# Latent attention: the softmax denominators of two query blocks are copied out by ScalarE, inverted by VectorE as 128 by 8 values and spread over partitions through DRAM

## The reference, cut to what matters

```
def attend(q, k, v):
    s = jnp.einsum('bqhgd,bkhd->bhgqk', q, k, preferred_element_type=jnp.float32) * (HEAD_DIM ** -0.5)
    p = jax.nn.softmax(s, axis=-1).astype(v.dtype)
    return jnp.einsum('bhgqk,bkhd->bqhgd', p, v)
...
    k_all = jnp.concatenate([kc, kl], axis=1)
    v_all = jnp.concatenate([vc, vl], axis=1)
    y_lat = merge(blocked_attention(ql, k_all, v_all), gal, fourier_mix(ul, f_gain, w_fmix), gbl)
```

## Time and profile before

| | |
|---|---|
| median of 3 runs | 3614.19 us (3607.61 to 3617.55) |
| profiled execution | span 3604.0 us; the page gives no other time for it |
| latent attention | about 690 to 1790 us of the span |
| DVE L2456, reciprocal | 24 times, 80.6 us |
| DVE busy over the span | 2375.8 us, 66% |
| ACT busy | 1357.8 us, 38% |
| PE busy | 3380.0 us, 94% |

### The profile page before, as it was taken

The page is one execution under the profiler, slowest core; times in us unless marked ns, Lnnn a source line. Parts: engine busy times, 40 slices in busy tenths (PEclk is TensorE's granted clock), DMA queues, the critical chain, the costliest instruction groups (busy, mean ns, idle before and its releaser), DMA issues. The chain is left out here.

```text
span 3604.0 us, 49705 instructions
## 1 busy us (share of the span) xinstructions
PE 3380.0 (94%) x16176; PEld 2490.9 (69%) x16176; DVE 2375.8 (66%) x3519; ACT 1357.8 (38%) x2274; POOL 1822.6 (51%) x1224
## 2 busy tenths in 40 slices
PE   7999998799999999999889799799999998999798
PEld 5788885555555555555488699687878786877587
DVE  4666544778877777777757654466575645777566
ACT  3433335444444444444320133234343423654200
POOL 1033313477777777777534344333686513444354
PEclk8999998899999999999999899999999999999899
DMA  5335545411111111111255455564545446777563
GB/s 204 116 109 142 142 135 187 147 33 35 36 36 35 36 36 35 35 36 35 94 171 175 160 185 177 181 201 148 170 134 170 152 149 208 219 224 238 191 224 138
DMA packets 358832, 475.35 MB, mean 132 GB/s; under 512 B 57932, under 2 KB 212444, under 8 KB 358512
## 3 DMA queue, kind: packets, MB, share of 16 engines
q1 hardware_dynamic: 300592, 358.80, 32.0%
q10 hardware_dynamic: 51600, 94.16, 8.6%
q0 software_dynamic: 6448, 19.94, 1.4%
HBM read 337.32 MB, written 135.36 MB: 131 GB/s over the span
## 5 line engine op out<-in xcount | busy, mean ns | idle before, releaser
L2413 DVE TENSOR_REDUCE al_mx<-al_sx 128x1 f32<-128x512 f32 (+1 forms) x960 | 559.3, 631 | 202.6 <-PE al_sx L2516 193.2
L2333 ACT ACTIVATE al_e<-al_st 128x1024 f32<-128x1024 f32 x432 | 442.8, 1026 | 536.1 <-PE al_st L2531 534.3
L2382 POOL TENSOR_TENSOR al_acc_p<-al_acc_p,al_e 128x1024 f32<-128x1024 f32 x188 | 455.3, 2422 | 19.8 <-POOL al_acc_p L2382 0.9
L319 PE MATMUL pb_acc<-p_whi,pb_r_hi 128*128 128x512 f32 x952 | 379.0, 398 | 38.7 <-DVE pb_r_lo L1767 28.1
L2540 PE MATMUL al_acc<-al_e,vres 128*64 128x512 f32 x1728 | 402.6, 601 | 0.0
L321 PE MATMUL pb_acc<-p_whi,pb_r_lo 128*128 128x512 f32 x952 | 376.4, 395 | 0.0
L320 PE MATMUL pb_acc<-p_wlo,pb_r_hi 128*128 128x512 f32 x952 | 375.8, 395 | 0.0
L1767 DVE TENSOR_TENSOR pb_r_lo<-pb_stg,pb_r_hi 128x512 fp32r<-128x512 f32 x238 | 247.5, 1043 | 167.6 <-ACT pb_r_hi L1665 163.4
L2530 PE MATMUL al_st<-al_qa,kres 128*128 128x512 f32 x864 | 346.8, 401 | 3.8 <-issue 3.2
L2531 PE MATMUL al_st<-al_qb,kres 128*128 128x512 f32 x864 | 341.0, 395 | 0.0
L2516 PE MATMUL al_sx<-kres,al_qx 128*128 128x512 f32 (+1 forms) x960 | 311.5, 398 | 9.1 <-DVE al_mx L2413 6.9
(11 more groups left out here) (340 smaller groups left out, 7387.0 us busy)
## 6 DMA issues: line engine op xcount, KB each, us to landing
pb_stg<-s_hsum ACTq DMA_DIRECT2D x238, 256.0 KB, 2.8
s_proj<-pb_out SPq DMA_DIRECT2D x72, 256.0 KB, 3.3
p_wst<-in_w1s ACTq DMA_DIRECT2D x18, 1024.0 KB, 5.9
ml_k<-s_proj SPq DMA_DIRECT2D x36, 512.0 KB, 4.4
ml_v<-s_proj SPq DMA_DIRECT2D x36, 512.0 KB, 9.0
hm_w<-in_ada_w SPq DMA_DIRECT2D x16, 1024.0 KB, 7.9
ml_qt<-s_qt SPq DMA_DIRECT2D x32, 512.0 KB, 6.4
s_h<-ml_h POOLq DMA_DIRECT2D x32, 512.0 KB, 8.4
```

The lines of the kernel that those rows point to most:

```text
L319: nc.tensor.matmul(out, s_hi, m_hi, start=start, stop=False)
L2333: nc.scalar.activation(e[:, pair(p, j), :, :], st[(NP * p + j) % 2][:, :, 0:W], ACT.Exp).then_inc(e_done, 1)
L2382: nc.gpsimd.tensor_tensor(acc_p[:], acc_p[:], e[:, pair(p, j)], ALU.add).then_inc(add_p, 1)
L2413: V.tensor_reduce(mx[:, x:x + 1], slots[x % NSX][:, 0:spans[x % NS][1]], AX.X, ALU.max).then_inc(sx_max, 1)
```

## The change

The sum over the partitions stays. What follows it is another chain, for every pair but the last, which keeps the old form:

1. ACT copies the 128x512 PSUM result into `den` between its exponentials of steps 7 and 8 of the even block, waits for its own copy, and issues two DMAs that each lay one row of 512 denominators over 64 partitions by 8.
2. DVE inverts 128x8 values in the turn of the odd block, after the maxima of step 2.
3. SP stores them to DRAM (`s_rden`), waits until they have landed, and issues two loads that spread one row of 512 each over 64 partitions.
4. DVE's `norm` waits for these loads instead of the reciprocal. PE's waits on `rden_done` become waits on `den_out`, the end of ACT's copy.

```diff
+            def spread(v):
+
+                sp.wait_ge(few_done, v + 1)
+                sp.dma_start(s["rden"].rearrange("i (p c) -> (i p) c", c=8), few[:, 1, :]).then_inc(few_st, 16)
+                sp.wait_ge(few_st, v * 16 + 16)
+                if not (fixed(v) and v == 0):
+                    sp.wait_ge(o_done, v)
+                for i in range(2):
+                    sp.dma_start(rden[i * HD:(i + 1) * HD, :], s["rden"][i:i + 1, :].broadcast_to([HD, W])).then_inc(rden_ld, 16)
...
+                if p == 1 and not (fixed(n) and n < 2):
+                    spread(v - 1)
                 if LAT and nxt is not None:
                     row(n + 1, 1 - p)
...
+            def sums_out(v):
+
+                act.wait_ge(den_mm, v + 1)
+                if not (fixed(v) and v == 0):
+                    act.wait_ge(few_ld, v * 32)
+                    act.wait_ge(few_done, v)
+                nc.scalar.activation(den[:], fo[:, 0:W], ACT.Copy).then_inc(den_out, 1)
+                act.wait_ge(den_out, v + 1)
+                for i in range(2):
+                    act.dma_start(few[i * HD:(i + 1) * HD, 0, :], den[i * HD:i * HD + 1, :]).then_inc(few_ld, 16)
...
                 for j in range(NP):
+                    if j == NP - 1 and p == 0 and not (fixed(n) and n == 0):
+                        sums_out(v - 1)
                     weights(n, p, j)
...
-                dve.wait_ge(den_mm, v + 1)
-                V.reciprocal(rden[:], fo[:, 0:W]).then_inc(rden_done, 1)
+                dve.wait_ge(few_ld, v * 32 + 32)
+                if not (fixed(v) and v == 0):
+                    dve.wait_ge(few_st, v * 16)
+                V.reciprocal(few[:, 1, :], few[:, 0, :]).then_inc(few_done, 1)
...
-                    if j == 8 and p == 0 and started:
+                    if j == 2 and paired:
                         inverse(v - 1)
...
-                    pe.wait_ge(rden_done, v - 1)
+                    pe.wait_ge(den_out, v - 1)
```

More of the change, by code:

```diff
@@ L2217, in attention @@
     asum, ot = m.sb(tag + "asum", [P, 2, W]), m.sb(tag + "ot", [P, W])
-    un, rden, o = (m.sb(tag + x, [P, W]) for x in ("un", "rden", "o"))
+    un, rden, o, den = (m.sb(tag + x, [P, W]) for x in ("un", "rden", "o", "den"))
+    few = m.sb(tag + "few", [P, 2, 8])
     even = m.sb(tag + "even", [HD, W])
@@ L2234, in attention @@
     stored = m.sem(tag + "stored")
+    den_out, few_ld, few_done, few_st, rden_ld = (m.sem(tag + x) for x in ("den_out", "few_ld", "few", "few_st", "rden_ld"))
     ctx_tr, ctx_out, ctx_stored = m.sem(tag + "ctx_tr"), m.sem(tag + "ctx_out"), m.sem(tag + "ctx_stored")
@@ L2453, in inverse, with norm @@
             def inverse(v):
-                dve.wait_ge(den_mm, v + 1)
-                V.reciprocal(rden[:], fo[:, 0:W]).then_inc(rden_done, 1)
-            def norm(v):
-                dve.wait_ge(rden_done, v + 1)
+                dve.wait_ge(few_ld, v * 32 + 32)
+                if not (fixed(v) and v == 0):
+                    dve.wait_ge(few_st, v * 16)
+                V.reciprocal(few[:, 1, :], few[:, 0, :]).then_inc(few_done, 1)
+            def norm(v, last=False):
+                if last:
+                    dve.wait_ge(den_mm, v + 1)
+                    dve.wait_ge(o_done, v)
+                    V.reciprocal(rden[:], fo[:, 0:W]).then_inc(rden_done, 1)
+                    dve.wait_ge(rden_done, 1)
+                else:
+                    dve.wait_ge(rden_ld, v * 32 + 32)
                 dve.wait_ge(un_done, 2 * v + 2)
@@ L2499, in _ @@
             joined(TOTAL - 1, 1, TOTAL // 2 - 1)
-            inverse(TOTAL // 2 - 1)
-            norm(TOTAL // 2 - 1)
+            norm(TOTAL // 2 - 1, True)
         @block.tensor
@@ L2547, in denominators @@
                 if not (fixed(v) and v == 0):
-                    pe.wait_ge(rden_done, v)
+                    pe.wait_ge(den_out, v)
                 for i in range(2):
@@ L3453, in program @@
         "attn": dram("s_attn", (QW, T)),
+        "rden": dram("s_rden", (2, 4 * P)),
         "x1": dram("s_x1", (T, D)),
```

## The result

| | before | after |
|---|---|---|
| median | 3607.51 us (18 runs, 3601.61 to 3617.55) | 3621.10 us (18 runs, 3607.29 to 3630.36) |
| profiled execution | span 3604.0 us | 3630.36 us, span 3628.6 |
| attention stage | 1050.41 us | 1062.31 us |

What follows compares the result with a forecast made beforehand. PE was taken to bound the attention stage. Eight straight turns at 0.26 us and 15 loop turns at 0.42 gave +8.4 us, all else 0: 3614.2 + 8.4 = 3622.6 us, range 3609 to 3634.

Steps and rivals of the forecast that it cites:

- the mechanism and its place: ACT between steps 7 and 8 of even turns: copy and two DMA issues delay step 8's exponential; +8.4 us.
- PE's waits for maxima: PE's loads before L2516 waiting for DVE's maxima, 30.2 us in 68 waits: upper bound of any gain, taken as 0.
- the formula in straight code: Even turns outside loops: step 8's exponential starts 0.75 us plus the two issues' time after the sums; loss 0.26 us each.
- z: Time in an even turn when the sums over the partitions are out, 1218.33 in the turn followed.
- D: Time ACT's queue is held by issuing the two DMAs: taken as 1.18 us, low 0.81, high 1.40.
- z + 1.67: Latest start of step 8's exponential, 1.67 us after the sums, at which PE still loses nothing.
- what I counted as 0: Removed reciprocals, 77.2 us of DVE, and the new chain through DVE, SP and DRAM: all under cover, 0 us.
- signs of being wrong: ACT issues under 0.45 or over 0.65 us each, odd turns changed, PE's maxima waits shrinking, or multiplication waiting for loads.
- the registers in loops: Register work on ACT ahead of the copy and ahead of the exponential: 0.08 us each, loss 0.42 in 15 loop turns.
- the crossing: Two DMA issues together taking 1.29 us on ACT, where the sum reaches the 0.3% line, 10.8 us.

Runs made afterwards that it cites:

- e1: Kernel before, reciprocal kept, plus only ACT's wait, copy and two DMAs whose results nothing uses: median 3618.63 us, ratio 1.0036, stage +11.77 us.
- e2: Changed kernel with one DMA of 128 partitions on ACT's queue in place of two: median 3602.94 us, ratio to before 0.9985, stage +0.11 us.
- e3: Changed kernel with both DMAs moved behind step 8's exponential, the copy left in place: median 3607.10 us, ratio to before 0.9999, stage +0.01 us.
- e6: Kernel before with a plain copy of the sums in place of DVE's reciprocal: median 3606.99 us, ratio 1.0000, stage +0.01 us.

## Why the prediction came out as it did

**Right: the mechanism and its place.** ACT's hold ahead of step 8 is all of the loss (e1 has all of it; e2 and e3 have none). Sign and sequence came out: exponential 8 starts 2.03 us after the sums (1.9 to 2.1 were named), the gap stands ahead of the fifth pair and is marked as waiting for ACT. PE's waits for maxima, in which I looked for a gain at most, are 29.3 us in 68 where they were 30.2 in 68.

**Right: the formula in straight code.** It starts at z + 0.75 + D with D = 1.28, 2.03 in the trace. The latest start without loss, z + 1.67, was worked out from the spacing of PE's pairs and an estimated 0.05 for the signal; the trace has 0.05 (1234.31 to 1234.36). 2.03 - 1.67 = 0.36, measured 0.36 to 0.43.

**Right: what I counted as 0.** The reciprocal (e6: +0.01 us), the short one (0.19 us into the idle 0.23), the store, its way through DRAM, the loads and the odd turns. The store landed in 1.4 us, where I took 2.3.

**Off: D.** I took 1.18 = 0.54 + 0.04 + 0.60. It is 1.25 to 1.30: in the loop turn shown, 0.47 for the first issue, 0.76 for the second and 0.03 between. The first was cheaper than I took, the second dearer than any row that I had (0.716). An issue over 0.65 us was one of the signs of being wrong that I named; the second issues are over it (0.75 to 0.79 in all turns but the first), the mean of a pair isn't. With 0.10 more in straight code and 0.09 in a loop, this term explains 8 x 0.10 + 15 x 0.09 = 2.1 us of what was missing. Why the second takes 0.76 wasn't settled. The row that speaks most is SP's: in this turn one of SP's issues runs from 1368.15 to 1368.75, beside the dear one. In e3, where ACT's pair came later, it took 0.47 and 0.62, and this time the load of queries that SP issued beside it took 0.69 us, where the same load takes 0.45 in the changed kernel. So issues of two queues may delay each other; no run took SP's away.

**Off: the registers in loops.** I took 0.08 us each ahead of the copy and ahead of the exponential. The trace has 0.13 ahead of the copy (1367.00 to 1367.13) and 0.25 behind the DMAs (1369.02 to 1369.27), where 0.12 + 0.08 was taken: 0.10 more in each of 15 turns, 1.5 us. With D's 2.1 that makes 8.4 + 3.6 = 12.0, against 12.3 measured in the even turns and 11.90 in the stage.

**Luck: the time itself.** I named 3622.6 us and 3621.10 were measured, but two errors cancel in that. I started from a median of 3 runs, 3614.2 us, where 18 runs give 3607.51, 6.7 less; and the medians lie 13.6 us apart instead of 8.4, 5.2 more.

**The side.** I had 0.53 on a change within 0.3% and 0.40 on slower. The ratio of 1.0035 lies just above that line and its interval on both sides of it. D came out at 1.27, hardly below the 1.29 that I named as the crossing; the registers did the rest. What decided the side, whether D lies nearer 1.2 or above 1.3, was the one open number, and no row of the trace before fixed it.

**The page that spoke against it.** The Trainium skill, "DMA: Bandwidth & Descriptors", section "Issuing engines are not separate DMA queues", calls a sequencer's time for starting a DMA usually small beside the DMA. Here 0.47 and 0.76 us stand beside a landing after 2.0. The measurement decides: it was a quarter to more than a third of the DMA, and for the queue that it holds, it was the whole loss. The 50 ns that the prediction took from the other section stand there for the GpSimd path, and these DMAs are issued by ScalarE.

## What to carry to other kernels

Work taken off an engine that nobody waits for was worth nothing here, though it was 77 us, and what it is replaced with can still cost: look first at what stands behind each new instruction in its queue, and who waits for that. A DMA issue that lays a row over many partitions held ScalarE's queue for about 0.5 us, and for 0.6 to 0.8 when it followed another, with little difference between 32, 64 and 128 partitions; merge the issues, or put them behind the operation that another engine needs. Either took the whole loss away, and neither made the stage shorter than before. And read the wait of the bounding engine for what stands ahead of it: moving one addition by three maxima gave 12.6 us of the stage, where the whole new chain gave nothing.

## What the runs showed of the hardware

- An issue on ACT's queue that lays rows over many partitions took, as the first of its kind in a row, 0.47 us for 64 partitions, 0.52 for 128 and 0.51 for 32. I had expected it to grow with the partitions.
- Of two issues in a row the second is the dearer one, 0.47 and then 0.76 (0.62 in e3, where they came later); of four, 0.51, 0.73, 0.61, 0.61.
- ACT's DMA issues run beside its own exponential when they stand behind it (e3), and hold it up when they stand ahead of it (after).
- The idle time behind the reciprocal was its slack to within 0.1 us: 0.93 us by the row; 3.39 us of further work made the next operation 2.38 us late.
- A DVE addition of 128x1024 values from two tiles in SBUF takes 1.21 us by itself. Begun while a POOL addition is under way, it ends 1.08 us after POOL's, up to 2.91 us after its start.
- A reciprocal of 128x8 values takes 0.191 us, one of 128x512 3.357. At 6.56 ns a value in the long one (3357 / 512), eight values are 0.05 us, so some 0.14 of the short one are fixed (an estimate).
